# A decoder step with sparse attention on one Trainium2 core: the prompt's value product takes two query heads behind one load of V, and the first cached values are gathered later

## What is computed

```python
def sparse_attend(q, ksel, vsel, valid):
    B, T, H, Dh = q.shape
    qg = q.reshape(B, T, N_KV_HEADS, H // N_KV_HEADS, Dh)
    s = jnp.einsum('btkgd,btnkd->btkgn', qg, ksel) * (HEAD_DIM ** -0.5)
    s = jnp.where(valid[:, :, None, None, :], s, -jnp.inf)
    p = jax.nn.softmax(s, axis=-1)
    o = jnp.einsum('btkgn,btnkd->btkgd', p.astype(vsel.dtype), vsel)
    return o.reshape(B, T, H * Dh)
```

## Time and profile before

| what | value |
| --- | --- |
| runs | 1155.5, 1158.72, 1158.74 us |
| median | 1158.72 us |
| span of the profiled execution, first to last instruction | 1155.7 us (its own time with what lies around the span isn't given apart) |
| PE busy | 1069.8 us, 93% |
| DVE busy | 570.3 us, 49% |
| ACT busy | 411.5 us, 36% |
| POOL busy | 242.8 us, 21% |

### The profile page before, as it was taken

One profiled execution on the slowest core, in us unless ns is written; L12 is line 12 of the kernel. 1 busy time (PEld: TensorE's weight loads), 2 busy tenths in 40 slices (PEclk: granted clock), 3 DMA queues, 4 the chain that ended last, 5 costly groups with the idle time before them and its releaser, 6 DMA issues. The chain is left out here.

```text
span 1155.7 us, 16387 instructions
## 1 busy us (share of the span) xinstructions
PE 1069.8 (93%) x6188; PEld 722.9 (63%) x6188; DVE 570.3 (49%) x1275; ACT 411.5 (36%) x973; POOL 242.8 (21%) x298
## 2 busy tenths in 40 slices
PE   6999999999998999999998998799999999999980
PEld 3643324554455677777786555486878787878760
DVE  4406699999988876666845641313111111111114
ACT  2325533978354455556531343111111111111114
POOL 4731116644411000000005110011212121212110
PEclk9999999999997999999998899899999999999995
DMA  8600000000192310111011771499999999999928
GB/s 267 229 18 1 1 18 1 9 30 5 41 246 91 125 56 27 48 38 56 27 60 64 279 284 69 157 367 344 328 335 344 333 345 334 340 337 342 278 33 318
DMA packets 51342, 191.42 MB, mean 166 GB/s; under 512 B 10926, under 2 KB 13950, under 8 KB 41029
## 3 DMA queue, kind: packets, MB, share of 16 engines
q1 hardware_dynamic: 39583, 142.71, 34.7%
q0 software_dynamic: 11536, 47.71, 14.6%
q10 hardware_dynamic: 158, 0.16, 0.1%
HBM read 162.49 MB, written 28.19 MB: 165 GB/s over the span
## 5 line engine op out<-in xcount | busy, mean ns | idle before, releaser
L1542 PEld LDWEIGHTS ps<-mem 128*128 128x128 f32 x2048 | 235.3, 193 | 16.8 <-issue 16.8
L1542 PE MATMUL ps<-mem 128*128 128x96 f32 x2048 | 234.8, 276 | 0.8 <-DVE mem L2538 0.8
L1618 ACT ACTIVATE mem<-ps 128x512 f32<-128x512 f32 (+7 forms) x338 | 149.4, 482 | 227.3 <-PE ps L1338 58.9
L2102 DVE TENSOR_SCALAR_CACHE_REDUCE mem<-mem 128x768 bf16<-128x768 f32 (+2 forms) x134 | 166.5, 1284 | 0.0
L1383 PE MATMUL ps<-mem 128*128 128x256 f32 (+1 forms) x544 | 125.5, 383 | 2.3 <-DVE mem L2391 1.3
L1548 PE MATMUL ps<-mem 128*96 128x512 f32 x256 | 119.3, 609 | 2.5 <-DVE mem L2530 2.5
L2530 DVE TENSOR_TENSOR mem<-mem,ps 128x192 f32<-128x192 f32 x32 | 11.4, 355 | 211.6 <-ACT mem L1978 211.6
L1383 PEld LDWEIGHTS ps<-mem 128*128 128x128 f32 (+1 forms) x544 | 98.8, 187 | 18.8 <-DVE mem L2402 2.6
L1021 POOL DMA_INDIRECT h_rows<-mem x32 | 46.5, 1454 | 296.6 <-DVE mem L2545 296.6
L1978 ACT ACTIVATE mem<-ps 128x192 f32<-128x192 f32 x32 | 10.6, 331 | 261.2 <-PE ps L1542 261.2
L1548 PEld LDWEIGHTS ps<-mem 128*96 128x96 f32 x256 | 39.5, 164 | 58.3 <-issue 52.4
(11 more groups left out here) (306 smaller groups left out, 1442.6 us busy)
## 6 DMA issues: line engine op xcount, KB each, us to landing
mem<-in_expert_w_gate SPq DMA_DIRECT2D x32, 1024.0 KB
mem<-in_expert_w_up SPq DMA_DIRECT2D x32, 1024.0 KB
mem<-in_expert_w_down SPq DMA_DIRECT2D x32, 1024.0 KB
mem<-in_x_prompt SPq DMA_DIRECT2D x16, 512.0 KB, 4.1
mem<-in_w_in SPq DMA_DIRECT2D x3, 2048.0 KB, 9.9
h_rows<-mem SPq DMA_DIRECT2D x8, 512.0 KB, 2.6
xn_rows<-mem SPq DMA_DIRECT2D x8, 512.0 KB, 2.9
mem<-h_rows SPq DMA_DIRECT2D x8, 512.0 KB, 5.4
```

Of the source, the lines that this page charges most:

```text
L1542: ins = mm(ps[:, 2 + s, j * CAP:(j + 1) * CAP], wgu[w][:, j // 2, k, (j % 2) * P:(j % 2 + 1) * P], xgT[:, s, k, :], start=(k == 0), stop=( ...
L1618: return fn(out, in_, ACT.Copy, scale=scale)
L2102: v.tensor_scalar(bufs[a % 3][0:R, 0:w], sc, mid[:, a:a + 1], None, ALU.is_ge, ALU.add, accum_out=cnt[:, a:a + 1]).then_inc(step, 1)
```

## The change

The value product is done at steps 1 and 3 only, for the step before and its own at once: the same V weights, and 256 moving columns, which are the turned probabilities of two heads side by side. For that the turned probabilities of two heads are kept: `PT` becomes `PTA` (2048 columns) and, for tiles 4 to 7, `PTB` beside it, which takes the place where the first gather of cached values lands. This gather is therefore issued later, behind the third of keys. `av_done` counts pairs of steps: the copies of an odd step no longer wait for the product before, those of an even step wait for the pair before. Nothing else in `tasks` is moved.

```diff
-        PT = cut(2 * 1024, (2, 8, P))
+        PTA = cut(2 * 1024)
...
+        PTB = mem[:, sc_at + 2 * SLOTS * P:sc_at + 3 * SLOTS * P]
...
+        def turned_probs(i, g):
+
+            if i < 4:
+                return PTA[:, 1024 * g:1024 * (g + 1)].rearrange("p (j h q) -> p j h q", j=4, h=2)
+            return (PTA, PTB)[g].rearrange("p (j h q) -> p j h q", j=8, h=2)
...
             past(Kin, ck_rows, 1, K_in)
-            past(Vin, cv_rows, 0, V_in)
             pool.wait_ge(admitted, 1)
...
             past(Kin, ck_rows, 2, K_in)
+            past(Vin, cv_rows, 0, V_in)
...
             def p_v(i, h):
-                if h == 0 and i:
+                if h % 2 == 0:
+                    return
+                if h == 1 and i:
                     pe.wait_ge(o_kept, i)
-                for c in range(0, i + 1, 4):
-                    for g in range(NKV):
-                        copied(pe, "2b", f"PT{pt_use['T', i, h, g, c]}", ("T", i, h, g, c))
+                for hh in (h - 1, h):
+                    for c in range(0, i + 1, 4):
+                        for g in range(NKV):
+                            copied(pe, "2b", f"PT{pt_use['T', i, hh, g, c]}", ("T", i, hh, g, c))
                 for j in range(i + 1):
                     for g in range(NKV):
                         half = slice(HD * g, HD * (g + 1))
-                        ins = mm(ps[half, 6, h * P:(h + 1) * P], V[:, j, half], PT[:, g, j, :],
+                        ins = mm(ps[half, 6, (h - 1) * P:(h + 1) * P], V[:, j, half], turned_probs(i, g)[:, j].rearrange("p h q -> p (h q)"),
                                  start=(j == 0), stop=(j == i))
                 ins.then_inc(av_done, 1)
...
-                        if i or h:
-                            act.wait_ge(av_done, i * PAIRS + h)
-                        copy(PT[:, g, c:c + n, :], ps[:, 4 + part, 0:n * P].rearrange("p (j q) -> p j q", q=P))\
+                        if i or h >= 2:
+                            act.wait_ge(av_done, i * (PAIRS // 2) + h // 2)
+                        copy(turned_probs(i, g)[:, c:c + n, h % 2, :], ps[:, 4 + part, 0:n * P].rearrange("p (j q) -> p j q", q=P))\
...
-                        act.wait_ge(av_done, (i + 1) * PAIRS)
+                        act.wait_ge(av_done, (i + 1) * (PAIRS // 2))
```

## The result

| | before | after |
| --- | --- | --- |
| median of four runs on one chip | 1158.73 us | 1174.44 us |
| lowest to highest | 1155.5 to 1159.4 | 1174.12 to 1176.05 |
| ratio, 95% interval | | 1.0139 [1.0121, 1.0157] |
| span of the profiled execution | 1155.7 us | 1172.4 us |

The change costs 15.7 us. The forecast was 1171.0 us (+12.3), with a range of 1163 to 1178. The two profiled executions differ by 16.7 us: in every run for which both are given the time is 1.8 to 2.0 us above the span, so the profiled execution of before took about 1157.6 us, 1.1 less than its median.

The account below looks back on a forecast made before the run. It took PE to pace the odd heads, and a DVE chain ending in the add to time the even heads as much as PE. Terms 14.8 - 1.05 - 0.8 - 0.9 + 0.2 = +12.3 gave 1171.0 us, range 1163 to 1178.

Parts of the forecast that it names:

- The fixed part of a block, 0.30 us: Per removed value-product block on PE: 0.16 us in it, 0.08 in front, 0.06 in the group behind.
- rival 1: Cover isn't needed: DVE empties bank M while PE streams, PE keeps 4.1 us, 1154.6 us; chance 0.09.
- Odd heads +14.8: Heads 1 and 3, tiles 1 to 7: 140 pairs each grow by 0.106 us on PE, +14.8 us.
- router wait -1.05: Head 3: the longer block swallows the router product's wait for DVE, 0.7 us plus 0.07 at five places.
- even heads -0.8: Heads 0 and 2: only PE's lateness behind DVE's add is won, 0.07 us mean at eleven places.
- tile 7's head 2 -0.9: Tile 7, head 2: DVE starts its maxima late; head 1's longer block gives that time back, -0.9 us.
- Tiles 0 and 1, +0.2: Up to 371 us DVE bounds: removed blocks give nothing, doubled ones cost little at half clock, +0.2 us.
- Rival 3: PE loses its clock in new waits of tiles 5 to 7, 1.4 us a stretch, 1174 to 1177 us; chance 0.18.
- The moved gather, 0: Later gather of cached values delays sample 3's keys, hidden by 0.2 us: 0, bounds 0 and +1.5 us.
- Nothing behind the attention absorbs a shift: Closing tasks, POOL's mask, samples and experts are a chain, each waiting for the one before.
- rival 2: Loads set a pair's pace, so 256 columns cost near 0.110 us: 1157 us or, halfway, 1164; chance 0.04.
- rival 4: Longer odd blocks let DVE recover at more even heads, 0.9 us each at most: 1164.5 to 1166.5 us; chance 0.08.

Follow-up runs that it names:

- experiment 3: The kernel before, with the value products of heads 0 and 2 taking only the first key tile; 1159.5 us, ratio 1.0009.
- experiment 4: The kernel after, with DVE's selection rounds of steps 0 and 2 moved behind its add of the output product; 1166.25 us, ratio 1.0077.
- experiment 2: The kernel after, with each double block doing its two heads one after the other at 128 columns, all 576 loads; 1173.62 us, ratio 1.0132.
- padded form of experiment 5: Experiment 5's kernel plus one matmul of padding before each turn of tile 0 and the first half of tile 1; 1164.31 us, ratio 1.0049.
- experiment 5: Experiment 4's changed kernel, with turned reciprocals moved behind step 1's first turn and the turned norm in another bank; 1165.51 us, ratio 1.0051.
- experiment 1: The kernel before, with only the first gather of cached values moved behind the third of keys; 1158.62 us, ratio 1.0004.
- experiment 6: Experiment 5's kernel, with ACT's squared norm of the older tile moved from step 0 to step 1; 1161.97 us, ratio 1.0031.
- the control of 4: The kernel before, with the same move of DVE's selection rounds behind its add; 1159.27 us, ratio 1.0009.
- experiment 7: Padding matmuls before turns of tile 0 and half of tile 1: kernel after 1173.54 us, before 1159.35, on experiment 5 1164.31, on experiment 6 1164.22.

## Why the prediction was right, and where it fell short

- *What bounds the stretch.* Right. The even steps are timed by the chain scores, maxima, selection round, add; experiment 3 shows it with 11.4 us of work against 0.6 us of time, experiment 4 from DVE's side. At the twelve even steps the next group starts 0.06 to 0.29 us behind the add in before and 0.05 to 0.06 in after.
- *Price of a pair of 256 columns, 0.216 us.* Right: blocks of 14 and 16 pairs take 3.26 and 3.69 us, 0.215 a pair, and all products 35.7 us at 256 columns and 36.0 at 128 (experiment 2). A saved load is worth nothing that shows.
- *The fixed part of a block, 0.30 us.* It enters only rival 1 (4.1 us with 0.004 a pair). PE's busy time in the stretch fell by 2.3 us in after, but by 3.8 in the padded form of experiment 5 (210.75 us at full clock), which has no wait for the add in front of the two groups. So the size holds; in after part of it doesn't show as long as PE stops behind each output product of an even step.
- *Odd heads +14.8, router wait -1.05, even heads -0.8, tile 7's head 2 -0.9.* Together +12.05. The 0.4 us of tile 1, step 1, lie before the second output product, so the sum says +11.6 for the stretch; measured +12.3. The router's wait is gone, the group behind an add starts 0.06 us behind it at all twelve places, and at tile 7, step 2, the wait is 1.03 us where the full chain of before would have made it 2.0: the 0.9 us came back as said. Not foreseen were the wait of tile 1 that grew by 0.8 us and the 0.6 us more before the turns.
- *Tiles 0 and 1, +0.2.* This is the step that failed: with the 0.4 us of tile 1's block +0.6 was due by the second output product, measured are +2.8, or +3.8 from the attention's own start. It priced the blocks there and took the clock as given. But the half clock ended 6.2 us later and took in the first output product, 6.45 us for 3.69. Rival 3 had the mechanism, a lower clock, and the wrong place: it put it behind the new waits of tiles 5 to 7, where the clock stayed at 1.00.
- *The moved gather, 0.* Right (experiment 1).
- *Nothing behind the attention absorbs a shift.* Right for the whole shift, since DVE's selection and POOL's mask come as late as the attention's end. But 1.5 us were added there, by the clock again, at half for 6.8 us instead of 3.4 over the samples' closing. Nothing of the change touches it: that router product takes 1.09 us in two other kernels with the change (with the round behind the add, and with padding) as in before, so chance is likely.
- *3.0 us around the span.* Wrong: 1.8 to 2.0 in every run. The profiled execution of before was a short one. The forecast doesn't suffer, as only the difference was added to the median.

The measured 1174.4 us is just above the 1167 to 1174 that had 0.61, in the band of rival 3, but not for rival 3's reason. Of the 16.7 us between the profiled executions 12.3 are explained and shown; about 4 are the clock's (2.8 under the first output product, 1.5 behind the samples). That the share at the start comes from the change is not settled. In five traces without padding that have the change's blocks (after, the narrow form, experiments 4, 5 and 6) it is 28.6 to 30.4 us from the first scores to the second output product, with 23.9 to 27.3 us of half clock; in four without the change (before, experiments 1, 3 and the control of 4) 26.5 to 28.6 us, with 17.1 to 23.9. Fewer or later matmuls in tiles 0 and 1 are a likely part of it, chance another; experiment 7 shows only that padding can take that half clock away.

Rivals 1, 2 and 4 are out: at no place was the bank free in time (experiment 3), loads set no pace (experiment 2), and DVE recovered at the one place that was counted.

## What to carry to other kernels

Before moving work off an engine that is 98% busy, look at what the work stands in front of: if the next group starts within 0.1 us of another engine's end, the work is cover, and its length is free where it stands and paid in full where it goes. Cover is rarely for one thing; here a 2 us product hid DVE's round, a bank's handoff and ACT's norm, and each had to be replaced before the loss was gone. Count what a change saves on the bounding engine first (here 2.3 to 3.8 us of 215): if that is small, no rearrangement behind it can win much.

## What the runs showed of the hardware

**The clock fell in one kernel and not in another over the same instructions behind the same wait.** Busy times where tile 2 ends and tile 3 begins, in experiments 5 and 6 (columns as above, the clock third from the end):

```profile
417.00:420.40 3.40, 3.40 (x11) 1.65 (x10) 1.01 (x4) 0.61 (x2) 0.00 (x0) 0.53 0.00 0
```

```profile
416.90:420.30 3.40, 3.40 (x17) 2.43 (x18) 1.61 (x6) 2.32 (x5) 0.00 (x0) 1.00 0.00 0
```

PE is busy throughout in both, behind a wait of 0.65 and 0.66 us; in 5 it runs at 1.2 GHz, in 6 at 2.4. Such a piece costs 1.7 us, and PE's waits from 376 to 425 us, which are the same in both, don't foretell it. The twelve new waits of after, up to 1.6 us each, cost no clock at all. The piece at 583.2 us in experiment 6, and that at 587.2 in its padded form, begin right behind two waits of 1.66 and 1.15 us; in experiment 5 the same two waits are 0.89 and 1.16 us, and the clock stays full. The Trainium skill, "TensorE: Matmul & The Clock Gate", section Part 1: The HAM clock gate (the "warmup" mystery), calls the number of matmuls that run cold run-variable, the same kernel showing different ones at its start. In this case the 28 runs of the kernel before agree, with a mean granted clock of 0.962 to 0.970; so, across kernels, do the two rows and the half clocks of the first tiles, which end at 367.0, 367.9, 370.0 and 373.2 us in kernels that are alike up to there or nearly so.

**A pair of fp32 value products is paid by its columns:** 0.110 us for 128, 0.215 for 256, at 576 or at 288 loads. The Trainium skill, "TensorE: Matmul & The Clock Gate", section Back-to-back issue gap, gives 81 ns a matmul at 128 columns and 131 at 512 in a stream of loads and matmuls; as an estimate from these, the wide pair would be 1.2 times the narrow one. The trace disagrees for this stream, with 1.95 times.
